# Latent attention's tiles in another order, two probability buffers, one gate scratch, and the stick-breaking opening by halves

## The reference

```
proj = h @ w_in                       # c_q 256, c_kv 128, k_rope 64, gate 2048
q    = (rmsnorm(c_q) @ w_uq)          # 16 heads x (128 + 64 rotary)
k, v = (rmsnorm(c_kv) @ w_ukv)        # 16 heads x (128, 128); k_rope shared
for each block of 128 queries:        # 8 blocks, keys 0..k_end only (causal)
    s = (q_nope k_nope + q_rope k_rope) * scale
    p = softmax(s);  o = p @ v
y = (o * silu(g)) @ w_out
```

## Time and profile before

| | us |
|---|---|
| median of 3 runs | 2547.23 (2547.14 to 2547.76) |
| the profiled execution | 2545.83 |
| its span, first to last instruction | 2544.1 |
| TensorE busy | 2343.1 (92%) |
| VectorE busy | 1572.1 (62%) |
| ScalarE busy | 1338.4 (53%) |
| GpSimd busy | 486.3 (19%) |
| mean granted TensorE clock | 0.979 of full |

### The profile page before, as it was taken

The page is one execution under the profiler, slowest core; times in us unless marked ns, Lnnn a source line. Parts: engine busy times, 40 slices in busy tenths (PEclk is TensorE's granted clock), DMA queues, the critical chain, the costliest instruction groups (busy, mean ns, idle before and its releaser), DMA issues. The chain is left out here.

```text
span 2544.1 us, 43259 instructions
## 1 busy us (share of the span) xinstructions
PE 2343.1 (92%) x17364; PEld 1324.1 (52%) x17364; DVE 1572.1 (62%) x2220; ACT 1338.4 (53%) x2013; POOL 486.3 (19%) x434
## 2 busy tenths in 40 slices
PE   8999998988788888988897899999999999999987
PEld 4667663444444445544453455554555446776643
DVE  5566675776656656655566566666665665667764
ACT  4444443445554445454543677777778643444442
POOL 0000111122112011111032133322332520011011
PEclk9999999998899999999999999999999999999999
DMA  3011112214333334343341211112111221111013
GB/s 118 26 43 43 42 37 89 73 48 83 75 79 80 87 65 90 72 90 77 91 102 52 65 43 49 52 51 59 43 46 39 75 68 35 40 46 34 35 61 122
DMA packets 198682, 160.32 MB, mean 63 GB/s; under 512 B 160306, under 2 KB 163122, under 8 KB 198484
## 3 DMA queue, kind: packets, MB, share of 16 engines
q1 hardware_dynamic: 194388, 153.36, 22.6%
q0 software_dynamic: 4096, 4.20, 0.7%
HBM read 98.79 MB, written 4.19 MB: 40 GB/s over the span
## 5 line engine op out<-in xcount | busy, mean ns | idle before, releaser
L240 PE MATMUL psum<-h_hi,w_hi 128*128 128x512 f16 x1128 | 429.9, 381 | 35.7 <-ACT mla_silu_g L285 18.5
L242 PE MATMUL psum<-h_hi,w_lo 128*128 128x512 f16 x1128 | 429.8, 381 | 0.0
L241 PE MATMUL psum<-h_lo,w_hi 128*128 128x512 f16 x1128 | 429.5, 381 | 0.0
L2408 DVE SCALAR_TENSOR_TENSOR w_lo<-wf,w_hi 128x1024 f16<-128x1024 f32 (+3 forms) x194 | 233.5, 1212 | 137.0 <-ACT w_hi L2403 137.0
L256 PE MATMUL psum<-w_hi,h_hi 128*128 128x128 f16 x1504 | 258.0, 220 | 0.0
L257 PE MATMUL psum<-w_lo,h_hi 128*128 128x128 f16 x1504 | 257.6, 220 | 0.0
L258 PE MATMUL psum<-w_hi,h_lo 128*128 128x128 f16 x1504 | 257.5, 220 | 0.0
L1681 ACT ACTIVATE ssum<-psum,mla_neg_top 128x128 f32<-128x128 f32 (+7 forms) x128 | 94.7, 740 | 298.3 <-DVE mla_neg_top L1588 298.3
L1140 POOL TENSOR_TENSOR sb_al<-sb_zc,sb_ah 128x256 f16<-128x256 f32 (+2 forms) x96 | 166.7, 1736 | 372.2 <-ACT sb_ah L1102 372.2
L2403 ACT ACTIVATE w_hi<-wf 128x1024 f16<-128x1024 f32 (+3 forms) x194 | 187.1, 975 | 41.9 <-PE psum L242 24.5
L240 PEld LDWEIGHTS psum<-h_hi,w_hi 128*128 128x128 f16 x1128 | 110.6, 98 | 156.6 <-issue 39.7
(11 more groups left out here) (332 smaller groups left out, 5839.5 us busy)
## 6 DMA issues: line engine op xcount, KB each, us to landing
wf<-in_gla_out SPq DMA_DIRECT2D x32, 512.0 KB, 3.5
wf<-in_sb_in SPq DMA_DIRECT2D x32, 512.0 KB, 3.5
wf<-in_mla_out SPq DMA_DIRECT2D x20, 512.0 KB, 3.6
wf<-in_gla_v SPq DMA_DIRECT2D x16, 512.0 KB, 3.5
wf<-in_gla_g SPq DMA_DIRECT2D x16, 512.0 KB, 3.5
wf<-in_mla_gate SPq DMA_DIRECT2D x16, 512.0 KB, 3.8
wf<-in_sb_out SPq DMA_DIRECT2D x16, 512.0 KB, 3.5
xT<-in_x_T SPq DMA_DIRECT2D x16, 256.0 KB, 5.3
```

The source lines that it names most:

```text
L240: pe.matmul(out, wh[:, w], act_hi[:, k, tok], start=(i == 0), stop=False)
L241: pe.matmul(out, wh[:, w], act_lo[:, k, tok], start=False, stop=False)
L242: mm = pe.matmul(out, wl[:, w], act_hi[:, k, tok], start=False, stop=(i == last))
L2408: dve.scalar_tensor_tensor(out=self.w_lo[s % Layer.NSPLIT][:, 0:cols], in0=self.wf[s % Layer.NLOAD][:, 0:cols], scalar=W_SCALE, in1=self.w ...
```

## The change

In the latent layer the item "m" loses its exponent, which becomes an item "e" of its own. Scores and maximum of a tile are placed one tile earlier, two ahead of the product, and the exponent of t + 2 lies behind the product of t - 1. There are two probability buffers, `net.ssum` and a new one, by the parity of the tile. The gate has one scratch. The copies of the rope queries for the next pair of heads are placed one tile earlier. In the stick-breaking layer the first pair is staged by halves: first query and key for tokens 0 to 511, each in its own staging half, then those for tokens 512 to 1023; and the last value unit comes before the first scores instead of after.

```diff
 class Gate:
-        self.buf = [L.sb(f"gate_tmp{i}", [P, HALF], F32) for i in range(2)]
+        self.buf = [L.sb(f"gate_tmp{i}", [P, HALF], F32) for i in range(buffers)]
-        if i >= 2:
-            dve.wait_ge(self.done, i - 1)
+        if i >= len(self.buf):
+            dve.wait_ge(self.done, i + 1 - len(self.buf))
 class StickBreaking:
-        for name, c in (("q", 0), ("q", 1), ("k", 0), ("v", 0), ("k", 1), ("v", 1)):
+        for name, c in (("q", 0), ("k", 0), ("q", 1), ("v", 0), ("k", 1), ("v", 1)):
...
-            if name in "qk":
-                out.append(("stack", name, 0, c))
-        return out[:-1], out[-1:]
+            if (name, c) == ("k", 0):
+                out += [("stack", "q", 0, 0), ("stack", "k", 0, 0)]
+            elif c and name in "qk":
+                out.append(("stack", name, 0, 1))
+        return out
+    def staging(self, name, p, c):
+        i = "qk".index(name) if p == 0 else c
+        return slice(i * HALF, (i + 1) * HALF)
-        items = [("start",)] + first + [("z", 0), ("lh", 0), ("ll", 0)] + values + [("z", 1)]
+        items = [("start",)] + self.first_items(w_in) + [("z", 0), ("lh", 0), ("ll", 0), ("z", 1)]
...
-                if name == "k" and p == 0:
-                    act.wait_ge((self.first_sent, self.staged_sent[0])[c], 128)
+                if p == 0:
+                    if c:
+                        act.wait_ge(self.first_sent, 192)
 class LatentAttention:
-            self.prob = net.ssum
+            self.probs = [net.ssum, sb("prob", [P, T], F32)]
-            self.gate, self.split = Gate(L), Split(L)
+            self.gate, self.split = Gate(L, buffers=1), Split(L)
-        items += [("s", 0), ("m", 0), ("d", 0)]
+        items += [("s", 0), ("m", 0), ("e", 0), ("s", 1), ("m", 1), ("e", 1), ("d", 0)]
...
-            main += [("s", t + 1), ("m", t + 1), ("gap", 1)] if t < last else []
+            main += [("s", t + 2), ("m", t + 2)] if t + 2 <= last else []
+            main += [("gap", 1)]
             main += [("pv", t - 1)] if t else []
+            main += [("e", t + 2)] if t + 2 <= last else []
             main += [("d", t + 1)] if t < last else []
-            if h % 2 and h + 1 < MLA_HEADS and 1 <= i < 5:
-                main += self.stage_items(h + 1, range(2 * i - 2, 2 * i))
+            if h % 2 and h + 1 < MLA_HEADS and i < 4:
+                main += self.stage_items(h + 1, range(2 * i, 2 * i + 2))
             main += [("gap", 1)]
...
-        elif kind == "m":
+        elif kind == "e":
...
             act.wait_ge(self.neg_ready, t + 1)
-            if t:
-                act.wait_ge(self.pl_ready, t)
+            if t >= 2:
+                act.wait_ge(self.pl_ready, t - 1)
```

More of the change, by code:

```diff
@@ L263, with __init__ @@
 class Gate:
-    def __init__(self, layer, taker="act"):
+    def __init__(self, layer, taker="act", buffers=2):
         L = self.layer = layer
         self.taker = taker
-        self.buf = [L.sb(f"gate_tmp{i}", [P, HALF], F32) for i in range(2)]
+        self.buf = [L.sb(f"gate_tmp{i}", [P, HALF], F32) for i in range(buffers)]
         self.clamped = L.sem("gate_clamped")
@@ L281, in act @@
         L, i = self.layer, self.order.index(n)
-        b = self.buf[i % 2][:]
+        b = self.buf[i % len(self.buf)][:]
         if self.taker == "act":
@@ L299, in dve_clamp @@
         L.wait_unit(dve, n)
-        if i >= 2:
-            dve.wait_ge(self.done, i - 1)
-        dve.tensor_scalar(self.buf[i % 2][:], out, -40.0, None, ALU.max).then_inc(self.clamped, 1)
+        if i >= len(self.buf):
+            dve.wait_ge(self.done, i + 1 - len(self.buf))
+        dve.tensor_scalar(self.buf[i % len(self.buf)][:], out, -40.0, None, ALU.max).then_inc(self.clamped, 1)
     def dve_mult(self, dve, n, out):
@@ L307, in dve_mult @@
         dve.wait_ge(self.sig, i + 1)
-        dve.tensor_tensor(out, out, self.buf[i % 2][:], ALU.mult).then_inc(self.done, 1)
+        dve.tensor_tensor(out, out, self.buf[i % len(self.buf)][:], ALU.mult).then_inc(self.done, 1)
     def wait_done(self, eng, n):
@@ L824, in build_items @@
         L = self.L
-        first, values = self.first_items(w_in)
-        items = [("start",)] + first + [("z", 0), ("lh", 0), ("ll", 0)] + values + [("z", 1)]
+        items = [("start",)] + self.first_items(w_in) + [("z", 0), ("lh", 0), ("ll", 0), ("z", 1)]
         filler = L.cut(self.projections(0, w_in, "g"), ("g",))
@@ L988, in dve @@
             if name in ("q", "k"):
-                self.split.dve(dve, n, self.st_hi[:, half], self.st_lo[:, half], self.scale_of(name))
+                at = self.staging(name, p, c)
+                self.split.dve(dve, n, self.st_hi[:, at], self.st_lo[:, at], self.scale_of(name))
             elif name == "v":
@@ L1056, in act @@
             if name in ("q", "k"):
-                if name == "k" and p == 0:
-                    act.wait_ge((self.first_sent, self.staged_sent[0])[c], 128)
+                if p == 0:
+                    if c:
+                        act.wait_ge(self.first_sent, 192)
                 elif name == "k":
                     act.wait_ge(self.staged_sent[p % 2], self.staged(p) - 64)
-                elif p >= 1:
-                    if p == 1:
-                        act.wait_ge(self.first_sent, 192)
+                else:
                     act.wait_ge(self.staged_sent[(p - 1) % 2], self.staged(p - 1))
-                self.split.act(act, n, self.st_hi[:, half], self.scale_of(name))
+                self.split.act(act, n, self.st_hi[:, self.staging(name, p, c)], self.scale_of(name))
             elif name == "v":
@@ L1163, in sync @@
             tokens = slice(halves[0] * HALF, (halves[-1] + 1) * HALF)
+            at = self.staging(name, p, *halves) if p == 0 else tokens
             sent = self.first_sent if a[2:] == (0,) else self.staged_sent[p % 2]
@@ L1172, in sync @@
                     sp.dma_start(dst[part * SB_DIM:(part + 1) * SB_DIM, p % 2, h, tokens],
-                                 src[rows, tokens]).then_inc(sent, 16)
+                                 src[rows, at]).then_inc(sent, 16)
 class LatentAttention:
@@ L1599, in dve @@
             ph = self.ph[t % 2]
-            dve.scalar_tensor_tensor(out=ph[:, w:2 * w], in0=self.prob[:, 0:w], scalar=self.inv_total[:, k],
+            dve.scalar_tensor_tensor(out=ph[:, w:2 * w], in0=self.probs[t % 2][:, 0:w], scalar=self.inv_total[:, k],
                                      in1=ph[:, 0:w], op0=ALU.mult, op1=ALU.subtract).then_inc(self.pl_ready, 1)
@@ L1676, in act @@
             act.wait_ge(self.neg_ready, t + 1)
-            if t:
-                act.wait_ge(self.pl_ready, t)
+            if t >= 2:
+                act.wait_ge(self.pl_ready, t - 1)
             if t >= 4:
                 act.wait_ge(self.inv_ready, t - 3)
-            act.activation(self.prob[:, 0:w], self.pair(t)[:, 0:w], ACT.Exp, bias=self.neg_top[:, k],
+            act.activation(self.probs[t % 2][:, 0:w], self.pair(t)[:, 0:w], ACT.Exp, bias=self.neg_top[:, k],
                            scale=self.SCALE, accum_out=self.total[:, k]).then_inc(self.p_ready, 1)
```

2 lines of the change are left out of this document (1 added, 1 removed).

## The result

The changed kernel takes 2517.28 us (median of four runs, 2515.41 to 2520.22) against 2547.49 us: a ratio of 0.9881, interval 0.9868 to 0.9894. That is 30.2 us less, where 80 were forecast; the time lies at the very edge of the stated range, just outside. The profiled execution took 2515.41 us, its span is 2513.7.

A forecast was written before the change was run, and what follows sets the result against it. TensorE, 92% busy, idles in latent attention because VectorE and ScalarE run late. 28 + 46 + 2 - 1 + 5.3 = 80 us off 2545.8, plus 1.4, gives 2467; range 2450 to 2487 (8 in 10: 2438 to 2517).

The forecast's parts named there:

- Part (a): Latent stage: ScalarE no longer waits at its queue's head for a maximum; the gate copy's 18.5 us of TensorE idle goes.
- Part (c): Latent tiles: maximum, exponent, high half, low half, next maximum stay serial; VectorE idles 14.4 us a head, 6 covered.
- Part (b): Latent stage: the division finds its exponent done a tile ago; the handoff (ScalarE idle 0.23 us) drops out.
- Part (d): Latent stage: possible new waits from score lag, buffers, gate scratch and earlier query copies on GpSimd's queue; taken as nothing.
- the opening: Stick-breaking's opening: first sum of logs 5.3 us earlier, from staging query and key by halves; bounds 3 to 8.
- the start: Latent start: two tiles instead of one filled before the first division, 1 us lost.
- head 15: Last latent head: 2 us of its waits gained.
- the gate scratch: Latent gate: with one scratch instead of two, the clamp does not wait for the earlier multiplication: nothing lost.
- rival B: Latent serial loop stays the bound; 7 us in heads 0 to 3, later only gate copies, 18.5: 2516; chance 0.20.
- C: Latent stage: almost all 114.5 us goes, clock staying 2.4 GHz in heads 0 to 3; 2435 us; chance 0.13.
- D: Latent tiles: late exponent holds banks, TensorE stands before each tile's scores; slower, 2595 at 1 us a tile; chance 0.05.
- E: Latent queues: their order makes no difference and nothing moves; 2542 from the opening alone; chance 0.02.

The follow-up runs named there:

- experiment 7: Changed kernel with the exponent of t + 2 directly behind its maximum, ahead of the first gap: 2537.64 us (0.9958).
- experiment 3: Changed kernel with ScalarE's and GpSimd's split of the gated product moved behind exponent and high half: 2496.34 us (0.9796).
- experiment 1: Changed kernel with the copies of the rope queries put back by one tile, to tiles 1 to 4 of an odd head: 2512.71 us (0.986).
- experiment 2: Changed kernel with both rope sums of an odd head ahead of all rope-query copies: 2496.35 us (0.9798).
- experiment 5: Changed kernel with the exponent of t + 2 behind the division of t + 1: 2492.21 us (0.9783).
- experiment 6: Changed kernel with division of t + 1, exponent of t + 2, product of t - 1 in this order: 2490.01 us (0.977).
- 4: Changed kernel with the exponent of t + 2 ahead of the product of t - 1: 2502.09 us (0.9819).
- experiment 11: Changed kernel with division, exponent, product in this order and both rope sums ahead of the copies: 2460.99 us (0.9658).
- 8: Kernel before with the stick-breaking part of the change alone: 2541.77 us (0.9978).

## Why the prediction was right or wrong

**Part (a), ScalarE no longer at the head of its queue before a maximum: the mechanism right, its cover wrong.** Experiment 7 puts it at about 20 of the 24 us that the latent part gained. The step that failed is "ScalarE is then free". It was said of maxima and believed of everything. The waits at the head of the queue moved: from 298.3 to 140.4 us at maxima (below 80 was named), from 18.6 to 125.3 at `mla_yt`. I had worked one even head with "pv" as a product on TensorE only, and so found 2 us to spare at each transpose; its ScalarE part, ahead of "e" and "d" in the new list, is the step that I left out. Its price is 21 us (experiment 3). With (c) this is why heads 4 to 14 gained 10.3 us of the 46 forecast.

**Part (b), the handoff: came true, and worth little alone.** VectorE's 70.1 us of waiting for exponents are gone, but experiment 7, which has that too, gained only about 5 us in this stage.

**Part (d), the copies on GpSimd's queue, "still three tiles ahead, 0": wrong.** I counted when the copies land, not what is queued behind their issue. The step moved four of them ahead of the rope sum on the same queue: 1.15 us of subtraction, four times 0.50 and the sum's own 1.27 make 4.4 us, and ScalarE stands idle for 3.52 of them. The gate copy is behind that, so part (a)'s 18.5 us came back as 16.2, in the odd heads alone. The copies are 9.1 us of it (experiment 1), the sum's place behind the subtraction the rest, and both together cost 21 us (experiment 2). The text itself had the condition ("If it were not free, its cover is gone and the price is the same 18.5") and gave it no weight.

**Part (c), the serial loop: seen, and under-priced.** VectorE's waits for high halves rose by 53 us instead of falling, which the prediction had named as a sign of being wrong. That the high half stands behind another tile's exponent is worth 25 us when undone (experiment 5), though part of that is the same lateness as `mla_yt`'s (experiment 6 gained 27 where 4 and 5 add to 40). Heads 0 to 3 gained 17.6 of 28, and the granted clock there reached 0.94 where above 0.95 was named.

**Do the terms close?** 21 (rope sums) + 27 (order, experiment 6) = 48, and 2517.3 - 48 = 2469; experiment 11, which has both edits, gave 2461. The clock has part of these 8 us. Heads 4 to 14 of experiments 6 and 11 (columns as in the earlier trace rows):

```profile
720.60:1245.38 524.78, 487.55 (x3506) 273.44 (x3505) 319.78 (x607) 265.02 (x486) 76.54 (x112) 0.98 0.39 86
716.03:1214.94 498.91, 478.90 (x3506) 271.92 (x3505) 319.93 (x607) 264.50 (x486) 76.99 (x112) 1.00 0.42 91
```

In experiment 6 the five stops on the gate copy stay, and the granted clock reads half for 17.1 us, beside four of them; the changed kernel has 17.1 us there too. Experiment 2 keeps 6.8 us, beside two waits for transposes of 2.4 and 2.9 us. Experiment 11 has no stop over 2 us in these heads and no half clock. So each edit alone leaves stops beside which the clock falls, and both together leave none. Had experiment 11 kept only the 6.8 us, it would be 3.4 us slower; the rest of the 8 is not broken down further.

That 2469 lies by the forecast of 2467 says little for the forecast. Experiment 11's heads 0 to 3 take 152.5 us where 148 was forecast, and its heads 4 to 14 take 498.9 where the forecast left 22 us over TensorE's 486.5, that is 508.5. The potential of the stage was read about right, from TensorE's own work, and the list of who stands where in each queue was not.

**Right**: the opening (6.0 and 5.8 against 5.3, from 11.94 us to the first scores against 11.85), the start (1.5 against 1), head 15, the gate scratch. Not foreseen: 3.2 us lost between the last product and stick-breaking's first, of which 1.5 are a TensorE wait at L395 for GpSimd's half of a split (1.75 before, 3.3 now).

**The rivals.** The measured 2517 is rival B's number (2516), but not its course: B let only the handoff go from heads 0 to 3 (7 us; 17.6 were measured) and all the gate copies' waits from the rest (18.5; five waits of 16.2 in all stayed). So B's number is luck, but its ground, the high half behind another tile's exponent, is what experiment 5 shows to cost. C's sum comes to about 109 us from its terms, not 112, and the forecast's unit of 0.0554 us stands in no row (the earlier trace rows gives 0.0558, 4 us more over these heads); neither changes the argument. D (scores before exponents) is 1.6 us in the changed kernel and shows only in the better orders, 10.5 us in experiment 11. E is out by experiments 7 and 8.

## What to carry to other kernels

When an item is moved in a list that several in-order engines share, write out for every engine what the item issues there, side effects on every fourth tile and DMA issues too, and for each of these what stands behind it and who waits for that. An idle engine by shares (ScalarE 53%) is no free engine: it stood 125 us before one operand, and moving only that operand's consumer on ScalarE and GpSimd gave 21 us. If an early wait is taken away, look where the same queue stops next, before the gain is counted.

## What the hardware showed that was not expected

A DMA issue holds GpSimd's own queue for 0.50 us (876.09 to 878.09 for four), and the rope sum behind them starts only when the last is issued. Sixteen of them are 8 us of that engine's queue per pair of heads. The page's busy time of GpSimd (481.2 us) has them in it: 128 issues, 63 us.

The low half 256 wide took 1083 ns beside GpSimd's subtraction. In head 0 of the kernel before, with the same buffer and nothing beside it, it took 0.48 us. In the changed kernel it takes 522 ns (650 to 1260 us: busy us, mean ns, idle before):

```profile
560.85 0.48 DVE L1600 SCALAR_TENSOR_TENSOR mla_prob_halves<-ssum,mla_inv_total,mla_prob_halves 128x256 f16<-128x256 f32 x1 [0.58 <-ACT mla_prob_halves L1689]
...
L1609 DVE SCALAR_TENSOR_TENSOR mla_prob_halves<-mla_prob,mla_inv_total,mla_prob_halves 128x256 f16<-128x256 f32 x12 | 6.3, 522 | 19.0 <-ACT mla_prob_halves L1698 19.0
```

So the neighbour doubled it. This is what the shared port pair of the Trainium skill (Trainium Architecture — The Big Picture, What this means for kernel authors) says, and the trace agrees on this width; the prediction had left it out of its sum. The overlap has not vanished, it starts later: the subtraction runs from 875.00 to 876.15 and the low half from 875.91 on. Before, the low half started 0.35 us after the subtraction and ended 1.43 us after that one's start; now it starts 0.91 us after it and again ends 1.43 us after its start. That is waiting for the neighbour and not sharing with it, and the wait ends about 0.2 us before the profile's end of the neighbour.

The low half 768 wide fits the same rule. It takes 1.02 us with nothing beside it, took 1.19 beside the subtraction before the change, and takes 1.43 beside a rope sum in seven heads of the changed kernel (the row at 953.92 above). In heads 0 to 3, where the prediction counted eight tiles at 0.5 us, four paid 0.6 and four 0.2. All in all such overlaps cost VectorE some 12 us before and 3.4 now, an estimate from these durations. It is small for an engine that idles 174 us for another reason.

Three of the five stops of TensorE of 3.24 us (at 780, 880 and 1080 us) are followed by 3.6 to 6.1 us of products at the lower clock (1.2 GHz of 2.4), 0.58 to 0.63 us each instead of 0.38; behind the other two the clock stays up. So taking the stops away gave back more than the stops: 21 us for 16.2.
